# A hybrid encoder block on one core: expert queries of all four token blocks in one pass over w_q, expert rows from step 8 on, turns four steps later

## The reference, cut to what matters

```python
# x: (1, 512, 1024) float32, one layer
h = rms_norm(x, norm_mix); proj = h @ w_in
x = x + (sigmoid(ga) * (attention(q, k, v) @ w_a) + sigmoid(gb) * (conv(cb, cc, cu) @ w_b)) @ w_out
# peer_ffn on rms_norm(x, norm_ffn), in blocks of 128 tokens
q = (x_blk @ w_q).reshape(n, 8, 2, 128)             # 16 lists of 128 numbers per token
s = einsum('nhpc,hpkc->nhpk', q, keys)              # 16 lists of 128 scores
top_s, top_i = top_k(s, 16)                         # per list
best_s, best_c = top_k(cand_s, 16)                  # of the 16 x 16 sums of a head's two lists
gate = softmax(best_s)                              # 8 heads x 16 experts of 16384 per token
act = gelu(einsum('nhkd,nd->nhk', expert_u[idx], x_blk))
y = einsum('nhk,nhkd->nd', gate * act, expert_v[idx])
out = rms_norm(x + y, final_norm)
```

## Time and profile before

| | us |
|---|---|
| median of 3 runs | 1656.71 (1655.1 to 1657.26) |
| the profiled execution, its own time | 1656.41 |
| its span in the trace | 1654.6 |
| PE busy | 1622.1 (98%) |
| DVE busy | 1289.2 (78%) |
| ACT busy | 790.3 (48%) |
| POOL busy | 786.6 (48%) |
| moved by DMA | 472.81 MB, mean 286 GB/s |

### The profile page before, as it was taken

One profiled execution on the slowest core, in us unless ns is written; L12 is line 12 of the kernel. 1 busy time (PEld: TensorE's weight loads), 2 busy tenths in 40 slices (PEclk: granted clock), 3 DMA queues, 4 the chain that ended last, 5 costly groups with the idle time before them and its releaser, 6 DMA issues.

```text
span 1654.6 us, 26240 instructions
## 1 busy us (share of the span) xinstructions
PE 1622.1 (98%) x10066; PEld 1450.6 (88%) x10066; DVE 1289.2 (78%) x2092; ACT 790.3 (48%) x937; POOL 786.6 (48%) x498
## 2 busy tenths in 40 slices
PE   8999999999999999999999999999999999999997
PEld 6878778889999999999999999998888888888886
DVE  3666622265997989999799689886778998989897
ACT  6454433336555565666667667633332323232323
POOL 4333334446864564544555545443275534544560
PEclk9999999999999999999999999999999999999999
DMA  5222223425638999999999999998999999999992
GB/s 166 77 75 77 76 77 89 115 81 143 193 119 303 415 348 344 349 328 327 331 359 415 417 382 389 388 349 310 346 369 396 396 395 395 394 397 393 394 392 117
DMA packets 247527, 472.81 MB, mean 286 GB/s; under 512 B 13824, under 2 KB 169504, under 8 KB 242080
## 3 DMA queue, kind: packets, MB, share of 16 engines
q1 hardware_dynamic: 173520, 253.52, 43.4%
q0 software_dynamic: 55296, 201.35, 31.5%
q10 hardware_dynamic: 18640, 17.06, 3.0%
HBM read 427.84 MB, written 44.04 MB: 285 GB/s over the span
## 4 chain that ended last, share of the span: by engine, by line
PE 66%; DVE 24%; DMA 5%; ACT 2%; issue 2%; POOL 1%; SPq 0%; ACTq 0%; DVEq 0%
PE psum L1483 23%; PE psum L320 16%; PE psum L1406 12%; DVE ring L1781 6%; PE psum L1385 4%; PE psum L1436 4%; DMA dg<-expert_gate 3%; PE psum L1394 2%; DVE acc L1786 2%; DVE cand L1099 1%; PE psum L539 1%; DVE hot L1768 1%; DVE hot L1771 1%; DVE hot L1769 1%; DMA ring<-in_expert_u,index 1%
## 5 line engine op out<-in xcount | busy, mean ns | idle before, releaser
L1650 POOL DMA_INDIRECT ring<-in_expert_u,index x256 | 378.2, 1477 | 388.3 <-DVE ring L1781 309.2
L1781 DVE SCALAR_TENSOR_TENSOR ring<-ring,x 128x1024 f32<-128x1024 f32 x256 | 306.1, 1228 | 59.0 <-DMA ring<-in_expert_u,index 59.0
L1406 PE MATMUL psum<-xnTh,uh 128*128 128x256 f32 x1024 | 300.0, 293 | 0.0
L1483 PE MATMUL psum<-vh,dwh 128*128 128x512 f32 x768 | 298.8, 389 | 0.0
L1483 PE MATMUL psum<-vl,dwh 128*128 128x512 f32 x768 | 298.8, 389 | 0.0
L1483 PE MATMUL psum<-vh,dwl 128*128 128x512 f32 x768 | 298.8, 389 | 0.0
L1406 PE MATMUL psum<-xnTl,uh 128*128 128x256 f32 x1024 | 289.5, 283 | 0.0
L1406 PE MATMUL psum<-xnTh,ul 128*128 128x256 f32 x1024 | 289.5, 283 | 0.0
L1558 ACT ACTIVATE vh<-v_raw 128x4096 fp32r<-128x4096 f32 x31 | 112.7, 3635 | 314.1 <-PE psum L1483 313.6
L1650 POOL DMA_INDIRECT ring<-in_expert_v,index x128 | 176.9, 1382 | 175.6 <-DVE acc L1786 141.1
L273 POOL TENSOR_TENSOR wl<-raw,wh 128x1024 fp32r<-128x1024 f32 x56 | 136.7, 2448 | 227.3 <-ACT wh L629 226.8
(11 more groups left out here) (259 smaller groups left out, 3063.4 us busy)
## 6 DMA issues: line engine op xcount, KB each, us to landing
u_raw<-in_expert_u SPq DMA_DIRECT2D x128, 512.0 KB, 6.7
v_raw<-in_expert_v SPq DMA_DIRECT2D x30, 2048.0 KB, 13.4
expert_gate<-grid SPq DMA_DIRECT2D x12, 2048.0 KB, 12.8
dg<-expert_gate SPq DMA_DIRECT2D x32, 768.0 KB, 21.3
raw<-in_w_in SPq DMA_DIRECT2D x40, 512.0 KB, 3.8
expert_act<-hb ACTq DMA_DIRECT2D x128, 128.0 KB, 6.1
dh<-expert_act SPq DMA_DIRECT2D x32, 512.0 KB, 14.2
raw<-in_w_q SPq DMA_DIRECT2D x27, 512.0 KB, 4.0
```

Of the source, the lines that this page charges most:

```text
L1406: last = nc.tensor.matmul(zb[s][:, 0:UT], w[s][:, c, :], x[:, c, 0:UT], start=(c == 0 and i == 0), stop=(c == C - 1 and i == 2))
L1483: last = nc.tensor.matmul(sums[k], w[s][:, j, b * P:(b + 1) * P], v[s][:, j, half * T:(half + 1) * T], start=(first and j == 0 and n == 0) ...
L1650: nc.gpsimd.indirect_dma_start(out=ring[k][:], out_offset=None, in_=tables[x // SLOTS], in_offset=bass.IndirectOffsetOnAxis(ap=numbers[x / ...
L1781: nc.vector.scalar_tensor_tensor(at, at, 1.0, of, ALU.mult, ALU.mult, accum_out=dots[:, k:k + 1]).then_inc(S["row_used"], 1)
```

## The change

One pass over `w_q`: 16 lists, each product 512 columns wide over all four blocks, two weight slots, loops in place of the written-out 31 lists. DVE ranks heads 0 to 6 of blocks 2 and 3 in the list stage, the eighth head in steps 0 to 2, then (step 3) scales x, finds the keys in steps 4 to 7, so rows start in step 8. All turns stand four steps later. `BY_VECTOR` shrinks from 15 to 11 tiles. `gate_in` and `exps` of blocks 2 and 3 move from the list stage to steps 5 and 8, those of blocks 0 and 1 stand two or three steps apart where they stood five or four. Five early `fetch`es no longer wait for PE's transposes.

```diff
-        for n in range(1, 2 * LISTS - 1):
-            project_list(n)
-            score_list(n - 1)
...
+        def query(i):
+            project(1, i + L5, xh, xl)
+            score_list(0, i)
+            project(0, i + (L5 + 1), xh, xl)
+            score_list(1, i)
...
-        for h in range(HEADS):
+        for h in range(HEADS - 1):
             dve.wait_ge(S["s_out"], h * 2 + 2 + PRIMED)
-            for k in range(PIECES):
+            for k in range(PIECES if h < HEADS - 2 else AHEAD):
                 rank(dve, h, k)
...
-TURN = (28, 68, 92)
+TURN = (32, 72, 96)
...
-RANK_STEPS = {0: tuple(range(0, 16)), 1: tuple(range(29, 48, 2))}
-KEYED = {0: (16, 17, 18, 20), 1: (49, 51, 53, 55), SPARSE: (57, 59, 61, 63)}
+FIRST_RANKS = (11, 14, 18, 22)
+RANK_STEPS = {0: tuple(range(8, 24)), 1: tuple(range(33, 52, 2))}
+KEYED = {MIXED: (4, 5, 6, 7), 0: (24, 25, 26, 28), SPARSE: (53, 55, 57, 59), 1: (61, 63, 65, 67)}
...
-GATED_IN = {17: (0,), 50: (1,)}
-EXPS = {22: (0,), 54: (1,)}
-GATED_OUT = {1: SPARSE, 2: MIXED, 25: 0, 64: 1}
-BY_VECTOR = range(113, STEPS)
+GATED_IN = {5: (MIXED, SPARSE), 25: (0,), 55: (1,)}
+EXPS = {8: (MIXED, SPARSE), 27: (0,), 58: (1,)}
+GATED_OUT = {10: SPARSE, 11: MIXED, 29: 0, 68: 1}
+BY_VECTOR = range(117, STEPS)
...
-IN_UP = 212
-AFTER_UP = (0, 3, 7, 11, 16, 21, 26, 32, 38, 44)
+IN_UP = 214
+AFTER_UP = (0, 3, 7, 11, 16, 21, 26, 32, 37, 42)
...
-    return sum((9 + 2 * len(SPREAD.get(i, ()))) * (14 if i < 30 else 11 if i < 64 else 12 if i < 110 else 7) for i in range(1, n + 1))
+    return sum((9 + 2 * len(SPREAD.get(i, ()))) * (13 if i < 34 else 10 if i < 68 else 13 if i < 114 else 7) for i in range(8, n + 1))
...
-    return min(3 * SLOTS, 2 * SLOTS + (z - LAST_DOT) * SLOTS // (2 * ROUNDS - 1 - LAST_DOT))
+    return min(3 * SLOTS, 2 * SLOTS + (z - LAST_DOT) * 6)
...
-            if 2 <= x < EARLY:
-
-                pool.wait_ge(ut_full[x % 2], (x + 2) // 2 + 1 + PRIMED)
```

More of the change, by code:

```diff
@@ L48 @@
 PRIMED = 1
+AHEAD = 11
 Q0, K0, V0 = 0, SBW, 2 * SBW
@@ L120, in mix_program @@
     wl = [m.put(f"wl{i}", 140 + 4 * i, [P, C, P], R) for i in range(3)]
-    late = m.put("raw2b", 92, [P, C, P]), m.put("wh2b", 96, [P, C, P], R), m.put("wl2b", 104, [P, C, P], R)
-    def list_tiles(n):
-        slot = list_slot(n)
-        return late if slot == 2 and n >= LISTS else (raw[slot], wh[slot], wl[slot])
     z = m.put("z", 152, [P, 2, ZW])
@@ L558, in last_rows, with score_list @@
                 pe.wait_ge(S["xT_lo"], 2 * C)
-        pe.wait_ge(S["xT_lo"], 2 * C - 1)
-        project_list(0, last_rows)
+            last = chunk(pj[0][:], 0, xh, xl, c, c, c == 0, c == C - 1)
+        last.then_inc(tile_done[0], 1)
         pe.wait_ge(S["key_ready"], LISTS // 4)
-        for n in range(1, 2 * LISTS - 1):
-            project_list(n)
-            score_list(n - 1)
-            if n == ROW_AT:
-                pe.wait_ge(S["row"], ROW1 + UB)
-                for b in range(UB):
-                    last = nc.tensor.transpose(av[:, b * P:(b + 1) * P], rb[:, b, :], ident[:])
-                last.then_inc(S["row"], 1)
+        def score_list(slot, i):
+            pe.wait_ge(taken[slot], i + (L4 + C // 2 + 1))
+            pe.wait_ge(S["s_out"], i * 2 + PRIMED)
+            at = slice(i * 2 + slot, i * 2 + slot + 1) if isinstance(i, int) else ds(i * 2 + slot, 1)
+            for b in range(NB):
+                last = nc.tensor.matmul(zt[slot][:, b * P:(b + 1) * P], ot[slot][:, b * P:(b + 1) * P],
+                                        keyT[:, at, :], start=True, stop=True)
+            last.then_inc(S["s_full"], 1)
+        def query(i):
[3 more added lines that the diff above has]
+            score_list(1, i)
+        with pe.Fori(0, 3) as i:
+            query(i)
+        pe.wait_ge(S["row"], ROW1 + UB)
+        for b in range(UB):
+            last = nc.tensor.transpose(av[:, b * P:(b + 1) * P], rb[:, b, :], ident[:])
+        last.then_inc(S["row"], 1)
+        with pe.Fori(3, LISTS // 2 - 1) as i:
+            query(i)
         pe.wait_ge(u_in[0], 16)
@@ L798, in mix_scalar @@
         act.wait_ge(S["oT_full"], C - 1 + PRIMED)
-        take_query(0)
-        high_list(3)
+        take_query(0, 0)
+        high(0, L4 + C // 2 + 1)
         act.wait_ge(S["oT_full"], C + PRIMED)
-        for n in range(1, 2 * LISTS - 1):
-            take_query(n)
-            if n + 3 < 2 * LISTS:
-                high_list(n + 3)
-            copy_list(n - 1)
-            if n == SQUARED_AT:
+        for i in range(LISTS // 2 - 2):
+            take_query(i, 1)
+            high(1, i + (L4 + C // 2 + 1))
+            copy_list(i, 0)
+            if i == 0:
                 act.wait_ge(S["x_added"], C + PRIMED)
@@ L1500, in experts_tensor @@
         down(1, ROUNDS - 1, final=True)
-    def exps(*blocks):
-        nc.scalar.preload_act_table_set("exp_and_others")
-        for b in blocks:
-            gates = sel[:, b, 2, :]
-            nc.scalar.wait_ge(S["exp_in"], EXP_ORDER.index(b) + 1)
-            nc.scalar.activation(gates, gates, ACT.Exp, scale=st[:, 3, b:b + 1]).then_inc(S["exp_out"], 1)
     def experts_scalar(act, last_list):
@@ L1534, in gelu, with exps @@
             act.dma_start(hv[:, n // 4:n // 4 + 1, n % 4, :], hb[n % 4][:].unsqueeze(1)).then_inc(h_out[n % 4], 16)
+        def exps(*blocks):
+            nc.scalar.preload_act_table_set("exp_and_others")
+            for b in blocks:
+                gates = sel[:, b, 2, :]
+                act.wait_ge(S["exp_in"], EXP_ORDER.index(b) + 1)
+                nc.scalar.activation(gates, gates, ACT.Exp, scale=st[:, 3, b:b + 1]).then_inc(S["exp_out"], 1)
         def keep(b):
@@ L1810, in weights @@
             nc.vector.tensor_tensor(w, w, dg[s][:, 0:UT // 32, :, :].rearrange("p b j n -> p j b n"), ALU.mult).then_inc(w_f[s], 1)
-        gate_in(MIXED)
-        gate_in(SPARSE)
-        for p in range(4):
-            keys(MIXED, p)
         for n in range(STEPS):
             if n == 0:
-                dve.wait_ge(scores_out, 2 * LISTS + PRIMED)
-                dve.wait_ge(x_made, 2 * C + C // 2)
+                dve.wait_ge(scores_out, LISTS + PRIMED)
+            if n < 3:
+                for k in range(FIRST_RANKS[n], FIRST_RANKS[n + 1]):
+                    rank(dve, HEADS - 2 + k // PIECES, k % PIECES)
+            elif n == 3:
                 for b, to, of in ((MIXED, x2, acc2), (SPARSE, x3, acc3)):
```

179 lines of the change are left out of this document (74 added, 105 removed).

## The result

| | us |
|---|---|
| after, median of 5 runs | 1671.08 (1667.28 to 1676.7) |
| before, median of 5 runs on the same chip | 1655.1 (1651.83 to 1657.26) |
| ratio | 1.0097, 95% interval 1.0079 to 1.0115 |
| the profiled execution of after, its own time | 1676.7 (span 1674.9) |

The forecast was 1649 us, with 1643 to 1662 around it.

The account below looks back on a forecast made before the run. PE's stream was taken to set the end. Steps -1.3 us (-11.7 + 1.8 + 0.8 + 7.8), lists -6.7 and half rounds +0.5 made -7.5 on the profiled 1656.4: 1649 us, range 1643 to 1662.

Parts of the forecast that it names:

- The list stage: Before the steps: lists of 6.35 us, no wait in the two-slot chain, step 0 at 484.6, 6.7 us sooner.
- DVE into the steps: From the lists to block 0's first batch: first row at 518, batch at 628, PE's step 34 at 629.2.
- block 0's wait: PE's 11.7 us lost to late DVE one-hots in steps 30 to 63 of before; forecast to go entirely.
- C: Rival: the list stage gives nothing, each of 14 lists waits 0.5 us for POOL or ACT; 1656 us, chance 0.12.
- E: Rival: ACT stops in step 27 or 58 for gate_in, costing PE 3 to 6 us; 1652 to 1656, chance 0.11.
- Where DVE is late next: new waits 7.8 us: From step 74 to the hand-over at step 116: PE waits 7.8 us more for DVE, range 6 to 11.
- Block 1's stretch, "no wait": Steps 74 to 89: DVE's lag reaches +10.2 us at step 90, 12.9 allowed, so PE does not wait.
- rival D: Rows late in both dense stretches, each of 78 rows costing DVE 0.2 us more; 1664 us, chance 0.24.
- Step 100 and the stretch behind, 3.9 and 2.4: From step 98: PE waits 3.9 us until DVE's lag is back at 12.9, then another 2.4.
- The hand-over, 1.5: At step 116, where DVE's low parts begin: lag shrinks to about +4 over two steps, PE waits 1.5 us.
- The early fetches without PE's transposes: Early row fetches, ungated: save DVE's waits only in steps where PE doesn't wait; nothing by themselves.
- Small terms: Low parts of four fewer tiles by DVE +1.8 us, exponentials with table loads +0.8, half rounds +0.5.

Follow-up runs that it names:

- e3: The changed kernel with thinner rows: 48 in steps 8 to 33, 59 in 34 to 67, 35 in 74 to 89, 36 in 98 to 113; 1.0093 of before.
- e10: The changed kernel with e2's turned slots and e3's thinner rows, the weights' hook left at row 211; 1.0032 of before.
- e14: e7 with the gate on POOL's row fetches extended to rows 2 to 43, two rows a tile; 0.9983 of before.
- e2: The changed kernel with the row ring's slots turned by two from row 203 on; 1.0127 of before.
- e1: The changed kernel with POOL's cast of the first down weights ahead of the fetch of row 213 instead of 211; 1.0105 of before.
- e4: The changed kernel with the edits of e1, e2 and e3 together; 0.9999 of before, 1652.94 us.
- e5: The changed kernel as it is, measured and profiled a second time; 1.0122 of before.
- e8: The kernel before without POOL's gate ahead of the fetches of rows 2 to 6, nothing else changed; 0.9984 of before.
- e6: The changed kernel with a gate put back on the fetches of rows 2 to 6, after the transposes of tiles 9 to 11; 1.0130 of before.
- e7: e4's three edits to the changed kernel plus e6's gate on the first fetches; 0.9978 of before, 1649.71 us.
- e13: The changed kernel with DVE's products for rows 0 to 43 cut to an eighth, fetches whole; profile only: eleven steps that should take 47 us took 70.2.
- e15: The kernel before with its gate on rows 2 to 6 replaced by one on rows 2 to 56, seven rows to three tiles; 0.9963 of before, 1648.57 us.

## Why the prediction was wrong, step by step

- **The list stage** held. Lists take 6.35 us as worked out, step 0 starts at 485.6 instead of 484.6, and the gain is 5.7 for 6.7. The chain of the profile of after:

```profile
425.36 5.47 PE psum L286 x24
430.83 0.89 PE psum L514 x8
```

- **DVE into the steps, and block 0's wait** held: first row at 519.4 (518 forecast), first batch at 626.71 (628), PE's step at 629.7 (629.2), and the 11.7 us are gone. Rivals C and E fall with it: no list waits, step 27 takes 4.2 us, and step 58 is 0.7 us longer than its neighbours, as the step of a table load is.
- **"Where DVE is late next: new waits 7.8 us" failed, and it is the main error.** In the profile of after PE's waits are 34.6 us. By its own parts:
  - *Block 1's stretch, "no wait"*: 6.8 us in steps 87 to 91. DVE's lag there wasn't the +10.2 forecast but +17.2 in step 88 and +15.0 in step 89, since DVE, which was to wait "for PE, not for rows", now waited five times for a row from 880 us on, 0.9 to 1.6 us each and 5.9 together. This is rival D's mechanism. That there was "no wait for a row there before" was misread too: DVE's timeline of before has two where block 1's stretch begins, 1.1 and 1.4 us ahead of the rows at 829.22 and 831.85. The DMA engines moved 400 GB/s at a share of 1.01: the extra rows did come faster than before's 392, as the sum had it, but not fast enough.
  - *Step 100 and the stretch behind, 3.9 and 2.4*: 6.3 and 4.7.
  - e3 shows that these three belong to the rows' density: with 35, 14 and 36 rows instead of 39, 15 and 39, all but 0.6 us of it was gone. It isn't the whole of step 100: e10 and e14 have the thinner rows too and lost 4.4 and 8.2 us there, with DVE 12.1 and 15.4 us behind at step 98. The row price that I used, 1.15 us of DVE, left out the waits for the row. (The 38.3 us for steps 90 to 97 takes 2.7 us for a row where the lines give 32.9 / 13 = 2.5; that is 0.4 us.)
  - *The hand-over, 1.5*: 8.0. The lag was forecast to shrink over two steps with one row each. Not priced was that the ring narrows at row 203, now in step 115 instead of 116, and that rows 203 and 204 wait for buffers of rows used two and three steps earlier, where it was four and five. e2, e3 and e10 show two causes in series, this and DVE's lag: with only one of them mended, 6 to 7 us are left. In e2 the cast ahead of row 205 has a part in what is left.
  - *Step 125, nothing forecast*: 8.8. I moved the rows in the sum and did not follow the hooks that are tied to a row's number. e1, e4 and e10 show it.
- **"The early fetches without PE's transposes ... nothing by themselves" failed** as to PE's stream. Where the gate is away, PE stalls: 4.6 us in e5's steps 8 and 9, 4.8 in e2, 7.2 to 7.6 in e1, e3, e4 and e10, 10 in e8's 4 and 5. What the gate is worth in whole time is another matter: e6, with a gate on the same five rows, was no faster than e5, e7 gained 0.2% on e4, and e8, the kernel before without its gate, was 0.16% faster than with it. The profile of after alone would have hidden it: it is the only one of nine with that front that shows no such stall.
- **Small terms** held within a microsecond: the low parts, the table loads, down (+0.6 for +0.5).
- **Rivals.** D was given 0.24 and 1664 us. It is the side on which the result fell, but the density of rows was only 17.8 of the 34.6 us; the rest was in no rival.

What stays open is how a run of fetches holds PE up. It isn't DVE's work (e13) and isn't the mean DMA share (e14, and the dense stretches from step 74 to 113, at about 1.0, where of all profiles only e1's has a signal over 0.2 us late, 1.5 us in step 94). Nor is it the number of fetches in a row alone: the profile of after has ten in a row and that of before eight, without a late signal, and e15 has threes and a short stall. Whether the clock falls first, unseen by the granted clock, or PE is starved first and the clock follows, these runs don't tell. Open too is why the stall in steps 8 to 33 differs so much between executions of one front: 0.3 us in the profile of after, 5.0 in e5 and 9.8 in e1, whose programs are the same up to row 210.
